# Chunk solve of an RWKV branch: merge products cut to the blocks of the triangular inverse that are nonzero

## What is computed

```python
def step(S, inp):
    r_t, w_t, k_t, v_t, a_t, b_t = inp
    sa = jnp.einsum('bhvk,bhk->bhv', S, a_t)
    S = (S * w_t[:, :, None, :] + sa[..., None] * b_t[:, :, None, :]
         + v_t[..., None] * k_t[:, :, None, :])
    return S, jnp.einsum('bhvk,bhk->bhv', S, r_t)
_, y = lax.scan(step, jnp.zeros((B, H, N, N), jnp.float32), xs)
```

## Time and profile before

| | us |
|---|---|
| time, median of 3 runs | 2063.66 (2061.09 to 2067.96) |
| the profiled execution, its own time | 2065.6 |
| its span in the trace | 2063.8 |
| PE busy | 1935.4 (94%) |
| DVE, ACT, POOL busy | 1140.2, 761.5, 691.2 |
| mean granted clock of PE | 0.961 |

### The profile page before, as it was taken

How to read it: one execution, slowest core, us unless ns; L and a number is a source line. 1 busy time by engine, 2 the same in 40 slices (tenths; PEclk the granted TensorE clock), 3 DMA queues, 4 the chain that set the end, 5 groups by cost and what they waited for, 6 DMA issues and landing times. The chain is left out here.

```text
span 2063.8 us, 26168 instructions
## 1 busy us (share of the span) xinstructions
PE 1935.4 (94%) x10724; PEld 1559.9 (76%) x10724; DVE 1140.2 (55%) x1417; ACT 761.5 (37%) x1114; POOL 691.2 (33%) x391
## 2 busy tenths in 40 slices
PE   8998999999999899999999999979989898999994
PEld 6777889988888677788998888848877784555552
DVE  6258755556675517865546667460026435666664
ACT  3345110333223343510133222342345635555552
POOL 0458210324444336721132444414420012333330
PEclk7999999999999999999999999989979998999997
DMA  7222300214453322220021544324310067999983
GB/s 310 94 90 73 102 1 1 93 62 152 176 184 141 113 92 92 76 78 1 31 83 62 198 180 160 126 83 142 133 41 1 12 264 259 352 348 340 344 295 131
DMA packets 78142, 284.62 MB, mean 138 GB/s; under 512 B 27283, under 2 KB 27411, under 8 KB 60740
## 3 DMA queue, kind: packets, MB, share of 16 engines
q1 hardware_dynamic: 71140, 272.36, 37.0%
q0 software_dynamic: 6144, 8.40, 1.1%
q10 hardware_dynamic: 736, 2.14, 0.3%
HBM read 274.44 MB, written 23.63 MB: 144 GB/s over the span
## 5 line engine op out<-in xcount | busy, mean ns | idle before, releaser
L1436 POOL TENSOR_TENSOR wmem_r<-wmem,wmem_r 128x1024 fp32r<-128x1024 f32 x170 | 420.4, 2474 | 667.6 <-ACT wmem_r L965 656.8
L652 PE MATMUL banks<-h_hi_r,wmem_r 128*128 128x512 f32 x1632 | 514.9, 395 | 13.6 <-POOL wmem_r L1436 7.6
L652 PEld LDWEIGHTS banks<-h_hi_r,wmem_r 128*128 128x128 f32 x1632 | 310.2, 190 | 82.8 <-POOL wmem_r L1436 9.2
L965 ACT ACTIVATE wmem_r<-wmem 128x1024 fp32r<-128x1024 f32 x170 | 180.2, 1060 | 482.1 <-DMA wmem<-wstream 479.3
L652 PE MATMUL banks<-hT_r,wmem_r 128*128 128x512 f32 x816 | 320.6, 393 | 0.0
L652 PEld LDWEIGHTS banks<-hT_r,wmem_r 128*128 128x128 f32 x816 | 155.3, 190 | 32.3 <-issue 0.5
L1998 PE MATMUL banks<-wmem_r,gm_mem_r 128*80 128x512 f32 x496 | 178.1, 420 | 0.0
L2520 POOL TENSOR_TENSOR wmem_r<-wmem,wmem_r 128x1024 fp32r<-128x1024 f32 x29 | 69.4, 2393 | 247.3 <-ACT wmem_r L2073 247.3
L1675 POOL DMA_INDIRECT y_tok_dram<-ztp,y_idx x32 | 66.5, 2077 | 221.4 <-DVE ztp L2446 215.0
L673 PE MATMUL banks<-wmem_r,h_hi_r 128*128 128x256 f32 x768 | 139.0, 284 | 0.0
L1377 DVE SCALAR_TENSOR_TENSOR ztp<-xT,c_act,ztp 128x256 f32<-128x256 f32 x168 | 124.8, 743 | 6.0
(11 more groups left out here) (409 smaller groups left out, 3430.6 us busy)
## 6 DMA issues: line engine op xcount, KB each, us to landing
wmem<-wstream SPq DMA_DIRECT2D x206, 512.0 KB, 3.6
slots<-experts SPq DMA_DIRECT2D x80, 1024.0 KB
xT<-ada SPq DMA_DIRECT2D x24, 1024.0 KB, 5.9
xT<-experts SPq DMA_DIRECT2D x16, 1024.0 KB
slots<-ada SPq DMA_DIRECT2D x8, 1024.0 KB, 18.3
x_keep<-xT SPq DMA_DIRECT2D x2, 2048.0 KB, 17.8
xT<-x_keep SPq DMA_DIRECT2D x2, 2048.0 KB, 8.8
dil_rows<-dil_once SPq DMA_DIRECT2D x1, 2560.0 KB
```

Of the source, the lines that this page charges most:

```text
L652: mm = nc.tensor.matmul(o, r(lhs[:, k, :]), r(rhs[:, k, :]), start=(k == 0 and i == 0), stop=(k == KD - 1 and i == 2))
L965: inc(nc.scalar.activation(r(chunk(b)[0]), w, ACT.Copy), "w_high")
L1436: inc(g.tensor_tensor(r(lo), lo, r(hi), ALU.subtract), "w_split")
```

## The change

The merge products are cut to the blocks that can be nonzero. At l=0 only the even 32-column blocks of P and T and the odd ones of Z are computed: the moving operand and the result have 64 columns a head in place of 128 and the stationary one keeps 128 columns. At l=1 only one 64x64 corner is computed: 64 rows, 64 stationary columns and 64 moving ones, and P goes into a corner of `tt`. DVE's operations on them have 256 elements per partition in place of 512 (at l=1 on 64 partitions, and the masking becomes a copy). The counts of instructions stay. As l=0 writes only the even blocks of `pt` and reads all of it, `pt` is cleared once per layer: POOL does it behind the splits of the `tg` chunks, and DVE waits for it (`p_clear`) ahead of the inversion. The table of masks shrinks from 256 to 64 columns.

```diff
@@ constants
-_names = [... ("lvl", NL * P), ...
+_names = [... ("lvl", 2 * SUB), ...
-    put("lvl", np.concatenate([((row // b) % 2 == 1) & (col // b == row // b - 1) for b in LEVELS], 1))
+    even = np.concatenate([i[2 * c * SUB:(2 * c + 1) * SUB] for c in range(2)])[None, :]
+    put("lvl", even // SUB == row // SUB - 1)
@@ views
+        pt_last = tt
+        HALF = P // 2
+        UPPER, LOWER = slice(0, HALF), slice(HALF, P)
+        sub_cols = lambda a, odd: a.rearrange("p u (c e j) -> p u c e j", e=2, j=SUB)[:, :, :, odd, :]
+        of_subs = lambda a: a.rearrange("p (u c j) -> p u c j", c=2, j=SUB)
@@ semaphores of a layer
-                          ("inv_spread", 16 * SUBS), ("z_clear", 4), ("z_init", NT * SUBS),
+                          ("inv_spread", 16 * SUBS), ("p_clear", 1), ("z_clear", 4), ("z_init", NT * SUBS),
@@ layer_tensor, the solve
-                            mm = nc.tensor.matmul(o[:, i * P:i * P + P], gm[:, u, 0, :], tt[:, u, :],
-                                                  start=True, stop=True)
+                            if l == 0:
+                                mm = nc.tensor.matmul(o[:, i * HALF:i * HALF + HALF], gm[:, u, 0, :], sub_cols(tt, 0)[:, u],
+                                                      start=True, stop=True)
+                            else:
+                                mm = nc.tensor.matmul(o[LOWER, i * HALF:i * HALF + HALF], gm[UPPER, u, 0, LOWER], tt[UPPER, u, UPPER],
+                                                      start=True, stop=True)
...
-                                mm = nc.tensor.matmul(o[:, i * P:i * P + P], zt[:, u, :], pt[:, u, :],
+                                mm = nc.tensor.matmul(o[:, i * HALF:i * HALF + HALF], zt[:, u, :], sub_cols(pt, 0)[:, u],
...
-                            mm = nc.tensor.matmul(o[:, i * P:i * P + P], pt[:, u, :], zt[:, u, :],
-                                                  start=True, stop=True)
+                            if l == 0:
+                                mm = nc.tensor.matmul(o[:, i * HALF:i * HALF + HALF], pt[:, u, :], sub_cols(zt, 1)[:, u],
+                                                      start=True, stop=True)
+                            else:
+                                mm = nc.tensor.matmul(o[UPPER, i * HALF:i * HALF + HALF], pt_last[LOWER, u, UPPER], zt[LOWER, u, LOWER],
+                                                      start=True, stop=True)
@@ layer_vector, before the inversion
             after("dg_gathered")
+            after("p_clear")
             for i in range(SUB - 1):
@@ layer_vector, the solve
-                        o = bank(f"p{n}{l}{g}").rearrange("p (u t) -> p u t", u=4)
-                        inc(v.tensor_tensor(flat(pt, g), o, mask, ALU.mult), "p_ready")
+                        o = bank(f"p{n}{l}{g}")[:, 0:4 * HALF]
+                        if l == 0:
+                            inc(v.tensor_tensor(flat(sub_cols(pt, 0), g), of_subs(o), mask, ALU.mult), "p_ready")
+                        else:
+                            inc(v.tensor_copy(flat(pt_last[LOWER], g)[:, :, UPPER], o[LOWER].rearrange("p (u t) -> p u t", u=4)), "p_ready")
...
-                            inc(v.tensor_tensor(flat(tt, g), o, flat(tt, g), ALU.add), "t_ready")
+                            inc(v.tensor_tensor(flat(sub_cols(tt, 0), g), o, flat(sub_cols(tt, 0), g), ALU.add), "t_ready")
...
-                        inc(v.tensor_tensor(flat(zt, g), o, flat(zt, g), ALU.add), "z_ready")
+                        if l == 0:
+                            odd = flat(sub_cols(zt, 1), g)
+                            inc(v.tensor_tensor(odd, of_subs(o), odd, ALU.add), "z_ready")
+                        else:
+                            corner = flat(zt[UPPER], g)[:, :, LOWER]
+                            inc(v.tensor_tensor(corner, o[UPPER].rearrange("p (u t) -> p u t", u=4), corner, ALU.add), "z_ready")
@@ layer_gpsimd
             low(FIRST["tg"], FIRST["pool_w"])
+            after("dg_stored", 8 * NT * SUBS)
+            inc(g.memset(pt, 0.0), "p_clear")
             after("inv_spread", 16 * SUBS)
```

More of the change, by code:

```diff
@@ L85 @@
     NGLOB += _w
-_names = [("mean", P), ("ones", P), ("freq", 64), ("eps", 1), ("ident", P), ("blk64", P), ("gram", W), ("lvl", NL * P),
+_names = [("mean", P), ("ones", P), ("freq", 64), ("eps", 1), ("ident", P), ("blk64", P), ("gram", W), ("lvl", 2 * SUB),
           ("ret_mask", W), ("ret_q", W), ("ret_k", 4), ("inv_count", 64), ("off", 2), ("causal", P),
@@ L1247, in layer_vector @@
                 for l in range(NL):
-                    mask = con("lvl")[:, l * P:l * P + P].unsqueeze(1).broadcast_to([P, 4, P])
+                    mask = con("lvl").rearrange("p (c j) -> p c j", c=2).unsqueeze(1).broadcast_to([P, 4, 2, SUB])
                     for g in range(2):
-                        o = bank(f"p{n}{l}{g}").rearrange("p (u t) -> p u t", u=4)
-                        inc(v.tensor_tensor(flat(pt, g), o, mask, ALU.mult), "p_ready")
+                        o = bank(f"p{n}{l}{g}")[:, 0:4 * HALF]
[3 more added lines that the diff above has]
+                            inc(v.tensor_copy(flat(pt_last[LOWER], g)[:, :, UPPER], o[LOWER].rearrange("p (u t) -> p u t", u=4)), "p_ready")
                     for g in range(2):
                         if l < NL - 1:
-                            o = bank(f"tn{n}{l}{g}").rearrange("p (u t) -> p u t", u=4)
+                            o = of_subs(bank(f"tn{n}{l}{g}")[:, 0:4 * HALF])
                             if l == 0:
@@ L1258, in layer_vector @@
                                 after("t_ready", 2 * (NL - 1) * n + 2 * (l - 1) + 1 + g)
-                            inc(v.tensor_tensor(flat(tt, g), o, flat(tt, g), ALU.add), "t_ready")
-                        o = bank(f"zn{n}{l}{g}").rearrange("p (u t) -> p u t", u=4)
+                            inc(v.tensor_tensor(flat(sub_cols(tt, 0), g), o, flat(sub_cols(tt, 0), g), ALU.add), "t_ready")
+                        o = bank(f"zn{n}{l}{g}")[:, 0:4 * HALF]
                         if l == 0:
```

## The result

The changed kernel takes 2158.39 us (2154.12 to 2170.39) against 2064.50 for the kernel before on the same chip: 94 us more, ratio 1.0462 with a 95% interval of 1.044 to 1.0485. Slower was forecast; the size, +26.6 us, was not: the time lies far above the range of 2080 to 2105.

What follows compares the result with a forecast made beforehand. PE was taken to bound the kernel: 35.4 us lost to the new wait plus 3.6 to the clock, less 12.4 won at l=1, gives +26.6 us, a median of about 2090 us, range 2080 to 2105.

Steps and rivals of the forecast that it cites:

- The new wait: DVE's wait for POOL's clear of `pt` ahead of the inversion: `ti` 17.3 and 18.1 us later, together 35.4 us lost.
- The rival of the slow inversion: Inversion on DVE doesn't get faster, taking 36.4 and 36.9 us again: sum +53, 2117 us; chance 0.06.
- l=0: Merge products with 64 moving columns: still 111 ns a record on PE, nothing won apart from gaps of 0.1 us.
- the rival of the faster l=0: 64 moving columns halve a product at l=0 too: 32.6 us won in all, sum +6.4, 2070 us; chance 0.06.
- l=1: Merge products cut to the 64x64 corner: 58 ns a record, 1.55 us less per chunk, 12.4 us in eight chunks.
- The clock: Behind each layer's new idle time PE runs some 3.6 us at 1.2 GHz, 1.8 us lost, 3.6 us together.
- The second rival below: Prediction's pointer for no DVE-POOL exclusion; second listed is 64 moving columns halving l=0 products: +6.4, 2070 us, chance 0.06.

Runs made afterwards that it cites:

- e1: The changed kernel, with DVE waiting for the clear of `pt` only behind the inversion, ahead of its first masked product: 2114.55 us, ratio 1.024.
- e6: The changed kernel with the late wait for the clear and l=0's products on PE 128 moving columns wide again, DVE's operations still short: 2058.18 us.
- e11: The changed kernel, early wait kept, with unneeded filler products ahead of each layer's first `ti` and in PE's 1.3 us gap of chunks n=1 to 3: 2091.55 us.
- e8: The changed kernel with the late wait and one unneeded product filling PE's 1.3 us gap at l=0 in chunks n=1 to 3: 2054.89 us.
- e7: The changed kernel, early wait and stall kept, with only l=0's products on PE made 128 moving columns wide again: 2098.49 us, ratio 1.0159.
- e2: The kernel before with only POOL's clear of `pt` and DVE's wait for it ahead of the inversion, all products wide: 2101.83 us, ratio 1.0193.
- e4: The kernel before with only l=1 cut to the 64x64 corner, without clear or wait: 2058.55 us, ratio 0.9983.
- e5: The changed kernel, early wait kept, plus seven unneeded products on PE ahead of the first `ti` of each layer: 2154.50 us, ratio 1.0429.
- e3: The changed kernel with the late wait and l=1 in full width again, so only l=0 is cut: 2091.51 us, ratio 1.0136.

## Why the prediction was wrong, step by step

**The new wait: right.** Inversion at 231.67 for 232.35, its length 23.33 for 23.4 us, `ti` 17.5 and 18.07 us late for 17.3 and 18.1. The rival of the slow inversion is out.

**l=0: right on time, blind on what it does to the clock.** 111 ns a record, as L813 of the kernel before had said; the rival of the faster l=0 is out. "So the moving half is worth nothing on PE" stopped there. It cost 56 us (e1 against e6; 59 by the differences).

**l=1: right, in part by luck.** 2.3 us at full clock for 2.16; 1.4 us less a chunk for 1.55. The forecast of 58 ns a record is what the trace shows, but the way to it was wrong. It took L766's mean of 77.5 ns as the price of 64 rows. A weight load with 64 rows and 128 stationary columns takes as long as one with 128 rows (lines of the kernel before, durations in ns as least, median and most):

```profile
L766 PEld LDWEIGHTS banks<-slots x512: 182/188/188, 243.7 to 986.5; 64*128 64x128 f32 x171
L782 PEld LDWEIGHTS banks<-ztp,gm_mem x256: 186/192/338, 250.1 to 998.7; 128*128 128x128 f32 x128
```

From load to load L766 needs 107 to 112 ns too, except around each switch to the next head, which lies in the other 64 partitions: there loads start in pairs, 1 to 5 ns apart, and this makes the mean of 77.5. So 64 rows by themselves are no cheaper; with half the stationary columns as well, l=1 takes 58 ns, about half of 111. The prediction said that the rule by columns leaves L766 out; the single loads agree with it.

**The clock: this is the step that failed.** The prediction took "once a layer" 3.6 us at 1.2 GHz behind the stall, 3.6 us of loss in all, with "nothing" and "twice that" as bounds, from the earlier trace rows, rows in which wide products follow the idle time. It carried the price of that recovery over to a kernel in which the products that would bring the clock back are just the ones that were made narrow. It also put the term behind the stall alone, though the fall in the earlier trace rows stands behind the gap of 1.2 us ahead of the second group of P, and this gap returns in three chunks of every layer: without the stall 131 of 151.5 us of low clock remain (e1). The low clock lasts 151.5 us in the two solves where 10.5 were before; half of the difference, 70 us, is an upper estimate of its price, as at half clock PE no longer waits for DVE. In the profiled executions the solves, from the first copy of `ti` to the last of `y`, are 64.3 us longer together than in e11, which keeps the clock, and the medians of the two kernels are 66.5 us apart (93.9 less 27.4).

With the clock kept, e11 is at +27.4 us, and the forecast's sum was +26.6. That they are so near is luck in part. In the profiled execution of e11 the time up to the first solve is 18.2 us longer and that between the solves 21.3 (17.3 and 18.1 forecast; 3.2 us between the solves are lost in e8 too, which has no stall), the solves are 15.8 us shorter together (8.8 forecast, low clock included), and 3.3 us are lost behind them. e7, with stall and l=1 cut and l=0 wide, is at +33.0.

**A slip.** "The second rival below", for the case that DVE and POOL don't exclude each other, is the first of the list, the slow inversion.

What each step costs in the changed kernel: the wait 39 us (e2, its own short recovery included), the cut of l=1 -4 to -7 (e4, e6), the narrow l=0 products about 60 (61 against e7), which is clock, as their records take no longer. They don't simply add up: the stall makes the first chunk slow and spares the second (e5).

What is shown: the gap left as it is (e8), narrow l=0 (e6) and narrow l=1 (e3) are each needed for the full loss. What is not settled: whether a filler with few columns would do as well, why, with wide products, the same gap brings the clock down for 3.4 us in 8 chunks of 30 and not at all in the others, and where 3.5 us of e4's gain go behind the solves.

## What to carry to other kernels

Where products get smaller and take the same time per instruction, ask what they do to the clock: price the stretch at 1.2 GHz too, and look for idle times of PE ahead of it. A recovery time read from the trace holds for the products that ran in it, not for those that replace them. A mean over a line's records can hide two kinds of them: look at single starts before a price is worked out from it. A helper's one-time clear belongs ahead of its first reader, not ahead of the longest job of that reader's queue; here its place alone costs 39 us.

## What the runs showed of the hardware

- PE at full busy share can stay at 1.2 GHz: 37.27 of 37.50 us busy, granted clock 0.50, with products of 64 moving columns in the main (144 of 198 records). The same products stay at 1.00 where they come behind `gram` products or fillers at full clock and PE's idle times between are 0.3 to 0.4 us, and one of 0.78 (e1's first chunk, e11).
- fp32 products of 128 rows and 128 stationary columns take 111 ns a record with 64 moving columns as with 128; at 1.2 GHz, with 64, 213. Those of 64x64 by 64 take 58. With 64 rows and 128 stationary columns it is 107 to 112 ns within one half of the partitions, and around a switch to the other half loads start in pairs, 1 to 5 ns apart (L766).
- A DVE operation with two SBUF inputs was stretched by 2.1 us under each POOL split before; without POOL's work beside it the inversion took 23.3 in place of 36.4 us. Operations that read PSUM and one SBUF operand aren't stretched: those of L1317 in the kernel before take 681 ns wholly under a split and 681 to 684 beside none. This is the exclusion that the Trainium skill, page "SBUF — State Buffer", section "Who interferes with whom", states, now shown by taking the other side away.
